# State-space decays from row-held running sums, multiplied out by wide matmuls

## The reference

```python
A_cs = jnp.cumsum(A, axis=-1)                     # A = dt * a, per head, chunks of 128 tokens
M    = CB[:, :, None] * jnp.exp(segsum(A))        # exp(A_cs[l] - A_cs[s]) for s <= l, else 0
y_diag = jnp.einsum("bgrcls,bcsgrp->bclgrp", M, X)
states = jnp.einsum("bclgn,bgrcl,bclgrp->cbgrpn", Bc, jnp.exp(A_cs[..., -1:] - A_cs), X)
y_off  = jnp.einsum("bclgn,cbgrpn,bgrcl->bclgrp", Cc, prev, jnp.exp(A_cs))
```

## Time and profile before

| what | us |
|---|---|
| median of 3 runs (lowest, highest) | 1012.22 (1010.21, 1019.31) |
| the profiled execution, its own time | 1012.6 |
| its span, first to last instruction | 1010.8 |
| PE busy / DVE busy / ACT busy / POOL busy | 953.0 / 668.2 / 500.0 / 135.9 |
| stretch of the state-space stage, k = 1 to 11 | about 264 to 398 |

### The profile page before, as it was taken

How to read it: one execution, slowest core, us unless ns; L and a number is a source line. 1 busy time by engine, 2 the same in 40 slices (tenths; PEclk the granted TensorE clock), 3 DMA queues, 4 the chain that set the end, 5 groups by cost and what they waited for, 6 DMA issues and landing times.

```text
span 1010.8 us, 18759 instructions
## 1 busy us (share of the span) xinstructions
PE 953.0 (94%) x7748; PEld 924.9 (91%) x7748; DVE 668.2 (66%) x922; ACT 500.0 (49%) x682; POOL 135.9 (13%) x97
## 2 busy tenths in 40 slices
PE   4399999899989999998999999999999999999998
PEld 4299999788889888998999999989998989999998
DVE  5855799988489998775856544453676655555542
ACT  2355654666577555343554533344668554444431
POOL 0500145300247863000000000000000000000000
PEclk9999999999999999999999999989999989999999
DMA  8755344566412225565654555536241335554650
GB/s 343 265 196 195 125 167 154 207 213 220 168 47 80 84 77 176 194 240 190 233 197 173 177 199 170 178 112 223 91 163 46 126 114 178 174 200 166 208 188 21
DMA packets 25086, 168.82 MB, mean 167 GB/s; under 512 B 2868, under 2 KB 4532, under 8 KB 4920
## 3 DMA queue, kind: packets, MB, share of 16 engines
q1 hardware_dynamic: 23616, 164.64, 46.9%
q10 hardware_dynamic: 1400, 3.16, 0.8%
HBM read 166.73 MB, written 1.06 MB: 166 GB/s over the span
## 4 chain that ended last, share of the span: by engine, by line
PE 80%; DVE 10%; ACT 4%; issue 3%; DMA 2%; POOL 1%; POOLq 0%; SPq 0%; DVEq 0%; ACTq 0%
PE bank L1621 78%; DMA raw<-w_stream 2%; DVE kw__107 L1226 2%; DVE acc L1012 1%; POOL sqs L457 1%; DVE wlo L989 1%; DVE yt L1247 1%; DVE sslo L1266 1%; DVE kw__107 L1232 1%; PE bank L1796 1%; ACT whi L513 1%; DVE yw L1256 0%; DVE hlo L1095 0%; DVE yt L1252 0%; DVE yt L1244 0%
## 5 line engine op out<-in xcount | busy, mean ns | idle before, releaser
L1621 PE MATMUL bank<-hhi,whi 128*128 128x256 f32 (+1 forms) x1384 | 403.8, 292 | 11.5 <-DVE hlo L1095 6.8
L989 DVE TENSOR_TENSOR wlo<-raw,whi 128x2048 fp32r<-128x2048 f32 (+1 forms) x131 | 301.1, 2299 | 158.7 <-ACT whi L513 158.6
L1621 PE MATMUL bank<-hlo,whi 128*128 128x256 f32 (+1 forms) x1384 | 395.9, 286 | 0.0
L1621 PE MATMUL bank<-hhi,wlo 128*128 128x256 f32 (+1 forms) x1384 | 395.7, 286 | 0.0
L513 ACT ACTIVATE whi<-raw 128x2048 fp32r<-128x2048 f32 (+1 forms) x132 | 250.2, 1896 | 94.3 <-PE bank L1621 67.4
L1621 PEld LDWEIGHTS bank<-hhi,whi 128*128 128x128 f32 (+1 forms) x1384 | 269.0, 194 | 19.4 <-issue 17.8
L1621 PEld LDWEIGHTS bank<-hlo,whi 128*128 128x128 f32 (+1 forms) x1384 | 269.3, 195 | 0.5 <-issue 0.2
L1621 PEld LDWEIGHTS bank<-hhi,wlo 128*128 128x128 f32 (+1 forms) x1384 | 268.9, 194 | 0.0
L1621 PE MATMUL bank<-fhi,whi 128*128 128x256 f32 x432 | 122.8, 284 | 0.0
L1621 PE MATMUL bank<-flo,whi 128*128 128x256 f32 x432 | 122.3, 283 | 0.0
L1621 PE MATMUL bank<-fhi,wlo 128*128 128x256 f32 x432 | 122.2, 283 | 0.0
(11 more groups left out here) (264 smaller groups left out, 1349.9 us busy)
## 6 DMA issues: line engine op xcount, KB each, us to landing
raw<-w_stream SPq DMA_DIRECT2D x156, 1024.0 KB, 4.9
xres<-x_t ACTq DMA_DIRECT2D x1, 1024.0 KB, 10.4
out<-oute SPq DMA_DIRECT2D x8, 128.0 KB, 3.3
tabs<-tabs_in_dram ACTq DMA_DIRECT2D x1, 641.0 KB, 5.6
tabs<-tabs_in_dram ACTq DMA_DIRECT2D x1, 512.0 KB, 3.6
hankel<-bucket_rows ACTq DMA_DIRECT2D x1, 512.0 KB, 5.3
cols<-cols_in_dram ACTq DMA_DIRECT2D x1, 325.0 KB, 13.3
tabs<-tabs_in_dram ACTq DMA_DIRECT2D x1, 64.0 KB, 13.0
```

The source lines that it names most:

```text
L989: nc.vector.tensor_tensor(out=wlo[:, c % RING, 0:n], in0=raw[:, r % RING, 0:n], in1=whi[:, c % RING, 0:n].bitcast(f32), op=ALU.subtract)\
L1621: return nc.tensor.matmul(out, lhsT, rhs, start=start, stop=stop)
```

## The change

The prefix sums of dt*A are made once, for all 64 heads-and-directions and both halves, as rows (head on the partition, token along the row): four f32 matmuls of `dta` against the two masks (256 columns, `side[3]`), placed after the k chunk. ScalarE copies them rounded to fp32r into partitions 0 to 63 and 64 to 127 of `csr`, VectorE puts the rest (exact minus rounded) into 64 to 127. Selector tables (`ind`, `dsel`, `gsel`, `ngsel`, `grp`) are made by VectorE in the convolution phase from the identity.

The decays of four heads of one direction are then two fp32r matmuls of 512 columns: a column of -1 at the group's rows against `bd` (each head's own row only, made by POOL once per token half and direction: `own_rows`), and `csr` against repeated identity columns. Forward and backward exponents are no longer added in one bank. They use the same banks one after the other: TensorE forward, ScalarE copies it out (`ew`), TensorE backward (after `states`), VectorE takes the maximum of the two (`later_decays`, two instructions a round, into `eb`), ScalarE one Exp of 1024 columns with scale -1. The edge decay is two matmuls of 512 columns. The rounds go by token half (i = 4t + g), so that `bd` is filled four times. `eb` lies where `acc` lies; for this modulation sum 8 moves from `so` to k = 1. POOL's mask products and `ax` are gone; per round it makes one copy of 64 columns (`group_halves`).

```diff
--- before.py
+++ after.py
+    rq0 = here[0]
     rq = place("rq", [P, NT, 20], f32)
     rqs = place("rqs", [P, NT, 20], f32)
-    ax = place("ax", [P, HG, HD], f32)
+    grp = place("grp", [P, 2, 3 * HD], f32r)
+    gsel = place("gsel", [P, NG], f32)
+    ngsel = place("ngsel", [P, NG], f32r)
     acc = place("acc", [P, 2, 512], f32)
     A0 = here[0]
+    eb = place("eb", [P, 2 * 512], f32, A0 - 4 * KB)
+    ind = place("ind", [P, 2 * NH], f32r, rq0)
+    dsel = place("dsel", [P, 2 * HG], f32, rq0 + 4 * 2 * NH)
+    csr = place("csr", [P, NT, P], f32r, tabs0 + 4 * TSPAN["gt"][0])
...
-    saf = place("saf", [P, HG, P], f32, TMP + 12 * KB + 256)
-    sab = place("sab", [P, HG, P], f32, TMP + 16 * KB + 256)
+    bd = place("bd", [P, 2 * HG, P], f32r, TMP + 12 * KB + 256)
...
-            def stationaries(i):
-                g, t = i // 2, i % 2
-                if i >= 1:
-                    pool.wait_ge(seg_done, i)
-                for dst, mask, d in ((saf, "gt", 0), (sab, "lt", 1)):
-                    a = dta[:, t, d * NH + g * HG:d * NH + (g + 1) * HG]
-                    nc.gpsimd.tensor_tensor(out=dst[:, :, :], in0=spread(tab(mask), 1, HG),
-                                            in1=spread(a, 2, P), op=ALU.mult).then_inc(sa_done, 1)
-                if i >= 1:
-                    pool.wait_ge(bc_done, i)
-                d = 1 - t
-                a = dta[:, t, d * NH + g * HG:d * NH + (g + 1) * HG]
-                nc.gpsimd.tensor_copy(ax[:, :, :], spread(a, 2, HD)).then_inc(ax_done, 1)
+            def own_rows(t, d):
+
+                nc.gpsimd.tensor_tensor(out=bd[:, d * HG:(d + 1) * HG, :],
+                                        in0=spread(csr[:, t, :].bitcast(f32), 1, HG),
+                                        in1=spread(dsel[:, d * HG:(d + 1) * HG], 2, P), op=ALU.mult)\
+                  .then_inc(bd_done, 1)
+
+            def group_halves(i):
+
+                if i >= 2:
+                    pool.wait_ge(bc_done, i - 1)
+                one = gsel[:, i % NG:i % NG + 1]
+                nc.gpsimd.tensor_copy(grp[:, i % 2, HD:2 * HD], bass.AP(
+                    tensor=one.tensor, offset=one.offset, ap=[list(one.ap[0]), [0, HD]])).then_inc(grp_done, 1)
...
+            pool.wait_ge(csr_done, 6)
+            pool.wait_ge(sel_done, 5)
+            own_rows(0, 0)
+            own_rows(0, 1)
             for i in range(8):
-                stationaries(i)
+                group_halves(i)
+                if i == NG:
+                    pool.wait_ge(segf_done, NG)
+                    own_rows(1, 0)
+                    pool.wait_ge(segb_done, NG)
+                    own_rows(1, 1)
...
+                    act.wait_ge(cst_done, 1)
+                    for part in range(2):
+                        for d in range(2):
+                            rows = slice(part * 2 * NH + d * NH, part * 2 * NH + (d + 1) * NH)
+                            nc.scalar.activation(csr[rows, :, :], side[3][rows, :].rearrange(
+                                "p (t d l) -> p t d l", t=NT, d=2)[:, :, d, :], ACT.Copy).then_inc(csr_done, 1)
...
             def iteration_exps(i):
-                act.wait_ge(seg_done, i + 1)
+                act.wait_ge(segf_done, i + 1)
                 if i >= 1:
-                    act.wait_ge(w_done, i)
+                    act.wait_ge(late_done, 2 * i)
                 for k in range(2):
                     nc.scalar.activation(ew[:, 4 * k:4 * k + 4, :].rearrange("p h l -> p (h l)"),
-                                         side[k][:, :], ACT.Exp).then_inc(ew_done, 1)
+                                         side[k][:, :], ACT.Copy).then_inc(sf_out, 1)
                 act.wait_ge(bc_done, i + 1)
                 if i >= 2:
                     act.wait_ge(sqs_done, i - 1)
-                nc.scalar.activation(yt[:, i % 2, :], side[4][:, :], ACT.Exp).then_inc(ebc_done, 1)
+                nc.scalar.activation(yt[:, i % 2, :], side[4][:, :], ACT.Exp, scale=-1.0).then_inc(ebc_done, 1)
+
+            def iteration_decays(i):
+
+                act.wait_ge(late_done, 2 * i + 2)
+                nc.scalar.activation(eb[:, :], eb[:, :], ACT.Exp, scale=-1.0).then_inc(eb_done, 1)
...
                 if 2 <= k <= 9:
+                    iteration_decays(k - 2)
                     iteration_weights(k - 2)
...
+                    dve.wait_ge(csr_done, 4)
+                    for d in range(2):
+                        rows = slice(2 * NH + d * NH, 2 * NH + (d + 1) * NH)
+                        nc.vector.tensor_tensor(out=csr[rows, :, :], in0=side[3][rows, :].rearrange(
+                            "p (t d l) -> p t d l", t=NT, d=2)[:, :, d, :], in1=csr[rows, :, :].bitcast(f32),
+                            op=ALU.subtract).then_inc(csr_done, 1)
...
+                if i == 2:
+
+                    dve.wait_ge(ident_in, 16)
+                    dve.wait_ge(rqx_done, 1)
+                    nc.vector.tensor_tensor(out=ind[:, :], in0=tab("ident")[:, 0:2 * NH],
+                                            in1=tab("ident")[:, 2 * NH:4 * NH], op=ALU.add).then_inc(sel_done, 1)
+                    dve.wait_ge(sel_done, 1)
+                    nc.vector.tensor_reduce(dsel[:, :].rearrange("p (d h) -> p d h", d=2),
+                                            ind[:, :].bitcast(f32).rearrange("p (d g h) -> p d h g", d=2, g=NG),
+                                            AX.X, ALU.add).then_inc(sel_done, 1)
+                    nc.vector.tensor_reduce(gsel[:, :], ind[:, :].bitcast(f32).rearrange(
+                        "p (d g h) -> p g d h", d=2, g=NG), AX.XY, ALU.add, negate=True).then_inc(sel_done, 1)
+                    dve.wait_ge(sel_done, 3)
+                    nc.vector.tensor_copy(ngsel[:, :], gsel[:, :]).then_inc(sel_done, 1)
+                    nc.vector.tensor_scalar(grp[:, :, :], tabs[:, 0:6 * HD].rearrange("p (a b) -> p a b", a=2), 0.0,
+                                            None, ALU.mult).then_inc(sel_done, 1)
...
+            def later_decays(i):
+
+                dve.wait_ge(segb_done, i + 1)
+                dve.wait_ge(sf_out, 2 * i + 2)
+                dve.wait_ge(modp_done, 9)
+                if i >= 1:
+                    dve.wait_ge(w_done, i)
+                for k in range(2):
+                    nc.vector.tensor_tensor(out=eb[:, k * 512:(k + 1) * 512], in0=side[k][:, :],
+                                            in1=ew[:, 4 * k:4 * k + 4, :].rearrange("p h l -> p (h l)"),
+                                            op=ALU.max).then_inc(late_done, 1)
+
             def decayed_products(i):
-                g, t = i // 2, i % 2
...
-                dve.wait_ge(ew_done, 2 * i + 2)
-                nc.vector.tensor_tensor(out=kw_[:, :, :], in0=kw_[:, :, :], in1=ew[:, :, :],
-                                        op=ALU.mult).then_inc(w_done, 1)
+                dve.wait_ge(eb_done, i + 1)
+                kw2 = kw_[:, :, :].rearrange("p h l -> p (h l)")
+                nc.vector.tensor_tensor(out=kw2, in0=kw2, in1=eb[:, :], op=ALU.mult).then_inc(w_done, 1)
...
+                if 2 <= k <= 9:
+                    later_decays(k - 2)
...
-                    modulation_out(16, 16, 8)
+                    modulation_out(16, 20, 9)
...
+                    masks = tabs[:, TSPAN["le"][0]:TSPAN["ge"][1]]
+                    for t in range(NT):
+                        for part in range(2):
+                            last = mm(side[3][part * 2 * NH:(part + 1) * 2 * NH, t * 2 * P:(t + 1) * 2 * P],
+                                      dta[:, t, :], masks)
+                    last.then_inc(cst_done, 1)
...
-                pe.wait_ge(sa_done, 2 * i + 2)
-                if i >= 1:
-                    pe.wait_ge(ew_done, 2 * i)
-                for h in range(HG):
-                    o = side[h // 4][:, (h % 4) * P:(h % 4 + 1) * P]
-                    mm(o, saf[:, h, :], tab("le"), True, False)
-                    last = mm(o, sab[:, h, :], tab("ge"), False, True)
-                last.then_inc(seg_done, 1)
-
-                pe.wait_ge(ax_done, i + 1)
+                decays(i, 0)
                 if i >= 1:
                     pe.wait_ge(ebc_done, i)
-                for j in range(4):
-                    a = ax[:, 2 * j:2 * j + 2, :].rearrange("p h d -> p (h d)")
-                    last = mm(side[4][:, j * P:(j + 1) * P], a, tab("ge" if t == 0 else "le"))
+                pe.wait_ge(bd_done, 2 * t + 2 - t)
+                pe.wait_ge(grp_done, i + 1)
+                for part in range(2):
+                    own = bd[:, (1 - t) * HG:(2 - t) * HG, :].rearrange("p (j two) l -> p two j l", two=2)[:, part]
+                    last = mm(side[4][:, :], grp[:, i % 2, HD - part * HD:HD - part * HD + P], own, part == 0, part == 1)
                 last.then_inc(bc_done, 1)
 
+            def group(g, n):
+
+                one = ngsel[:, g:g + 1]
+                return bass.AP(tensor=one.tensor, offset=one.offset, ap=[list(one.ap[0]), [0, n]])
+
```

(32 more changed lines are left out.)

28 lines of the change are left out of this document (12 added, 16 removed).

## The result

| us | before | after |
|---|---|---|
| median of 20 runs each (lowest, highest) | 1012.63 (1009.75, 1019.44) | 1007.98 (1002.80, 1010.64) |
| profiled execution, its span | 1012.6, 1010.8 | 1008.98, 1007.1 |
| last multiply of `kw_` begins | 382.29 | 379.56 |

The ratio is 0.9933 [0.9917, 0.9949]: 0.7% faster. Forecast were 1011.8 with a range of 1003 to 1020, and "within 1%" at 0.86; both hold. The sum foresaw a gain of 0.8 us and the median gives 4.6, so the terms are worth a look.

A forecast was written before the change was run, and what follows sets the result against it. VectorE was taken to bound the state-space stage, TensorE 1.3 us behind, and TensorE to bound the rest. Stage terms sum to -1.6, outside +1.7 and -0.9: 1012.6 becomes 1011.8 us, range 1003 to 1020.

The forecast's parts named there:

- 1, maxima +9.8: VectorE in the state-space rounds: two maxima per round, 1.40 us together, add 9.8 us over seven rounds, without a wait.
- 3, line 1247 -6.7: State-space rounds without POOL's mask products: line 1247 loses 6.7 us over five rounds, `sslo` 4.9 over four.
- 4, `own_rows` +1.3: POOL's remaining work: `own_rows` near line 1247 of k = 5 costs +1.3 (0 to +3.8), `xd` at `sslo` +2.1.
- 5, wide matmuls at 0.24: TensorE's rounds: ten 512-column fp32r matmuls at 0.24 us replace mask side work; the k = 4 wait goes, -1.6 us.
- 6, handshake 0: Each round's forward, copy, backward, maximum, Exp: TensorE is ready 2 us early (1.3 without `tat`), so nothing is charged.
- 7, third round +1.7: ScalarE's table load and Exp of `eb` ahead of VectorE's weights: +0.1 us at the start, +1.7 in the third round.
- step 2: First round: the eight instructions of line 1226, 5.86 us beside POOL's products, get shorter without them, -3.4 us.
- Step 9: Outside the state-space stage: four f32 prefix-sum matmuls cost +1.7 us; sum 8 leaving the so phase gives -0.9.
- A: State-space rounds: VectorE's blocked time only moves to other two-input instructions; 1020 us, or 1023; chance 0.14.
- C: Lean case in the state-space stage: POOL yields each time and ScalarE is not late; 1006 us, perhaps 1004; chance 0.16.
- D: State-space rounds: `xd` always starts ahead of `sslo`, which waits for all of it; +4.2, 1013.9 us; chance alone 0.2.
- E: TensorE waiting longer per round in the stage drops to half clock, +1 to +3 us; chance inside the forecast's 0.62.

The follow-up runs named there:

- no_max: The changed kernel with each of the two maxima cut to 32 of 512 columns, backward decays left out; 1004.1 us, ratio 0.9914 to the kernel before.
- moved: The kernel after with 448 bytes left free in front of A0, restoring the old addresses from there on; 1009.49 us, ratio 0.9953 to the kernel before.
- xd_later: The kernel after with POOL's `xd` waiting, from the third round on, for the first maximum; 1004.39 us, ratio 0.9892 to the kernel before.
- pool_place: The kernel after with second-half `own_rows` for direction 0 moved to the fourth round and `xd` waiting for the first maximum; 1004.3 us, ratio 0.9900.

## Why the prediction was right, and which terms were not

The likeliest case held: a little faster, within 1%. That the sum came within 4 us of the median is in part luck: several terms of 1 to 4 us that no step had, of both signs, are listed below. By the prediction's steps, in the rounds first (forecast +9.8 - 6.7 - 4.9 + 2.1 + 1.3 - 1.6 + 1.7 = +1.7, measured +2.4):

- **1, maxima +9.8**: 7 x 1.2 = 8.4, and 1.5 of wait for TensorE at k = 3, in a stretch of half clock. 9.9 together, but not for the stated reason: its sum had no wait at the maxima and named one as a sign that it is wrong. One came, in one round of seven.
- **3, line 1247 -6.7**: right, 1.14 in every round without `own_rows`. **`sslo`** with `xd`: -4.9 + 2.1 = -2.8 foreseen; in four rounds 0.88 and three times 1.52 against 2.17, -3.2.
- **4, `own_rows` +1.3**: 2.55 (3.69 - 1.14), inside its bounds of 0 to 3.8. The choice of "what line 1247 lost before" was too low: line 1313 (317.75 to 321.44) was caught by both instructions (316.18 to 319.98) and by `xd` behind them.
- **5, wide matmuls at 0.24**: confirmed. The timeline of TensorE has four of them from 265.82 to 266.80, 0.245 each, and the two with `grp` behind them take 0.47 up to the next product at 267.27:

```profile
265.82 0.48 PE L1689 MATMUL bank<-bd,ngsel 128*128 128x512 f32 x1
...
266.80 0.63 PE L1689 MATMUL bank<-bd,grp 128*128 128x512 f32 x2
```

  The wait for `outputs_own` of k = 4 went (-1.6).
- **6, handshake 0**: right but for k = 3. no_max shows how thin the cover is.
- **7, third round +1.7**: 1.77. The timeline of ScalarE there:

```profile
304.07 0.58 ACT L730 ACTIVATE st<-bank 128x512 f32<-128x512 f32 x1
304.66 1.28 ACT L724 ACT_TABLE_LOAD   x1
305.96 1.06 ACT L724 ACTIVATE eb<-eb 128x1024 f32<-128x1024 f32 x1
```

  `st` ends at 304.65 and Exp starts 0.02 us after the load. The drain of 1.38 us that the Trainium skill, page ScalarE: Activation LUTs, section What ACT_TABLE_LOAD costs, adds to a switch is not seen; an estimate by it would put the wait at 1.77 + 1.38, about 3.1.

Of the other signs: the heads (line 1307) of k = 5 to 8 are 16.4, 13.9 and 13.7 us apart (316.31, 332.72, 346.59, 360.32), the first outside the forecast 13.3 to 14.4 by `own_rows`; TensorE's waits for `cbb` are up to 3.8 us, not about 2.

Ahead of the rounds, forecast -3.4 (step 2), +0.1 (7) and +1.7 (9): -1.6; measured -5.2. **Step 2** is right (5.86 to 2.33). **Step 7** held: load and Exp take 2.26 (277.02 to 279.28), `products(0)` is 3.1 us shorter, and sum 8 stands in front of it and costs its 0.9 (the lead of 1.7 at 260 us is 0.9 at 265.57):

```profile
262.65 0.95 PE L1689 MATMUL bank<-onec,acc 128*128 128x1 f32 x8
```

**Step 9 failed in size.** The prefix sums cost 1.0, not 1.7: eight rows in 1.02 us, each with a half of the columns (128*64), which fits pairs of them running side by side:

```profile
81.78 1.08 PE L1689 MATMUL bank<-tabs,dta 128*64 128x256 f32 x8
82.80 0.39 PE L1689 MATMUL bank<-hhi,whi 128*128 128x256 f32 x1
```

Yet Silu's table load comes 4.0 us earlier (271.81 for 275.82), not 0.5. The rest belongs to no step, as the starts of ScalarE's weight splits show (before and after): 78.02 and 77.35, 0.7 won already ahead of the prefix sums (0.35 of it at the first split); 88.99 and 89.44 behind them, then 110.74 and 109.57, 1.6 won, where one half-clock stretch near 100 us is 3.4 us shorter in this execution; 183.15 and 181.98, then 194.12 and 192.45, another 0.5, where TensorE's wait for `prob` is 1.32 instead of 1.68. **Step 8** held: 397.76 became 395.04, with the path.

Behind the stage the forecast had -0.9 and nothing else; sum 8 gave some 1.0 there. Besides it the address shift gave -2.4 in the output phase and -2.0 in the second block's `fhi` stretch (splits at 574.43 and 571.00, then 662.09 and 656.65). Half clock took back some 1.5 us at 396.4 to 399.8, 3.0 at 700.3 to 707.1 (33 matmuls where the kernel before has 61) and 1.4 near 780. moved prices the shift: with the old addresses the change is worth 0.9953 instead of 0.9933; the intervals overlap, the paces do not. A diff of kernel code that also moves a buffer has a term that no step of mine had.

Of the rivals, **A** (relief does not come) is excluded, POOL's remaining work costs mainly where it meets instructions with two SBUF inputs. **B** is excluded by 0.24. **C**, 1006, is the nearest number, though for other reasons. **D** came true for `xd`: it started first three times and cost 0.84 each, not 1.05. The Trainium skill, page SBUF — State Buffer, section Who interferes with whom, says that the first to start keeps the pair for its whole instruction; `xd` 330.01 to 331.05 and `sslo` ending at 331.60, 0.55 later, agree. **E** came too, stronger than priced: the profiled execution has four half-clock stretches of 3.4 us between 283 and 400 us, where before had none. Over the 20 runs of the kernel after, the two with a mean clock of 0.985 took 1002.8 and 1002.9 us, the eleven at 0.976 took 1005.6 to 1009.9.

Still open: why half clock comes at 700 and 779 us, since TensorE is busy there. Each kernel has one trace, so layout and execution cannot be told apart: xd_later has stretches at both places and pool_place, with the same layout, none, but pool_place's profiled execution is its fastest (998.64 us, mean clock 0.988, the other six 0.974 to 0.981). Open too is the second condition of the pace.

## What to carry to other kernels

When VectorE is the bound, look first at what POOL does while VectorE reads two SBUF operands: the same instruction at two prices in one trace is the sign, and moving POOL's operation beside an instruction that reads PSUM cost nothing here. Taking POOL's products away paid for two maxima a round here, and nothing more; a rewrite that adds to the engine in the critical round spends the gain it brings. Before crediting a small change of time to the mechanism, look at the pace of code that was not touched: one moved buffer can be worth as much.
